# Sixteen bytes: weight rows and moving rows at another distance in SBUF

## What is computed

```python
x = x + rms_norm(mixers(rms_norm(x) @ w_in) @ w_out)
x = x + rms_norm((gelu(gate) * val) @ ffn_down)       # gate, val = split(causal_dwconv(rms_norm(x) @ ffn_up))
x = x + 0.5 * (silu(h @ w_gate) * (h @ w_up)) @ w_down   # h = rms_norm(x), twice, with d_ff = 5632
x = x + branches(attention(rms_norm(x) @ w_in_2)) @ w_out_2
```

## Time and profile before

| | |
|---|---|
| time, median of 3 runs | 3365.83 us (3364.95 to 3367.11) |
| profiled execution | 3365.98 us, of it the span 3364.2 us |
| TensorE matmuls busy | 3345.9 us, 99% |
| TensorE weight loads busy | 2933.9 us, 87% |
| VectorE busy | 2240.1 us, 67% |
| ScalarE busy | 1746.2 us, 52% |
| GpSimd busy | 533.2 us, 16% |
| granted TensorE clock | full throughout |

### The profile page before, as it was taken

One profiled execution on the slowest core, in us unless ns is written; L12 is line 12 of the kernel. 1 busy time (PEld: TensorE's weight loads), 2 busy tenths in 40 slices (PEclk: granted clock), 3 DMA queues, 4 the chain that ended last, 5 costly groups with the idle time before them and its releaser, 6 DMA issues.

```text
span 3364.2 us, 59341 instructions
## 1 busy us (share of the span) xinstructions
PE 3345.9 (99%) x19746; PEld 2933.9 (87%) x19746; DVE 2240.1 (67%) x2874; ACT 1746.2 (52%) x2588; POOL 533.2 (16%) x502
## 2 busy tenths in 40 slices
PE   9999999999999999999999999999999999999999
PEld 8888888888888888888888888888888888888888
DVE  7879587777744566556555599766687655656544
ACT  5555665555544554545444555554565554554443
POOL 0214111111100011111100066511100111111000
PEclk9999999999999999999999999999999999999999
DMA  6534555555566555555566655545556555555665
GB/s 213 163 114 154 184 169 189 190 188 187 188 193 188 178 179 192 189 190 187 187 192 189 219 175 175 189 155 159 171 193 199 190 187 193 188 188 189 186 194 175
DMA packets 176036, 616.21 MB, mean 183 GB/s; under 512 B 20912, under 2 KB 21584, under 8 KB 175568
## 3 DMA queue, kind: packets, MB, share of 16 engines
q1 hardware_dynamic: 175520, 609.84, 56.2%
q10 hardware_dynamic: 432, 5.24, 0.4%
HBM read 610.81 MB, written 4.19 MB: 183 GB/s over the span
## 4 chain that ended last, share of the span: by engine, by line
PE 94%; DVE 3%; issue 1%; ACT 1%; DMA 1%; POOL 0%; DVEq 0%; SPq 0%; POOLq 0%; ACTq 0%
PE acc L463 59%; PE acc L466 30%; DVE weights_low L313 1%; PE ps_wide L392 1%; PE acc L478 1%; ACT weights_high L306 0%; PE ps_narrow L2552 0%; PE ps_wide L2528 0%; PE acc L481 0%; DVE halves_memory L568 0%; DMA weights_raw<-in_w_in 0%; DMA x_T<-in_x 0%; DVE halves_memory L3011 0%; DMA weights_raw<-in_w_diff_branch 0%; PE ps_scale L2933 0%
## 5 line engine op out<-in xcount | busy, mean ns | idle before, releaser
L463 PE MATMUL acc<-moving_halves,weights_high 128*128 128x512 f32 x6304 | 1981.0, 395 | 1.8 <-DVE x_T L2821 1.8
L313 DVE TENSOR_TENSOR weights_low<-weights_raw,weights_high 128x1024 fp32r<-128x1024 f32 (+1 forms) x1172 | 1432.8, 1236 | 719.8 <-ACT weights_high L306 718.6
L306 ACT ACTIVATE weights_high<-weights_raw 128x1024 fp32r<-128x1024 f32 (+1 forms) x1172 | 1209.0, 1033 | 773.1 <-PE acc L466 746.7
L466 PEld LDWEIGHTS acc<-moving_halves,weights_low 128*128 128x128 f32 x6304 | 1185.0, 188 | 269.0
L466 PE MATMUL acc<-moving_halves,weights_low 128*128 128x256 f32 x6304 | 1244.0, 279 | 0.0
L463 PEld LDWEIGHTS acc<-moving_halves,weights_high 128*128 128x128 f32 x6304 | 952.4, 188 | 12.0 <-issue 9.8
L463 PE MATMUL acc<-gated_halves,weights_high 128*128 128x512 f32 x2024 | 628.0, 392 | 0.0
L562 ACT ACTIVATE cross_products<-acc 128x256 f32<-128x256 f32 x503 | 192.9, 383 | 671.2 <-PE acc L466 671.1
L466 PEld LDWEIGHTS acc<-gated_halves,weights_low 128*128 128x128 f32 x2024 | 380.1, 188 | 83.8
L585 POOL TENSOR_TENSOR stage_scratch<-unscaled,token_scale 128x256 f32<-128x256 f32 x260 | 215.2, 828 | 1287.2 <-DVE unscaled L568 807.3
L466 PE MATMUL acc<-gated_halves,weights_low 128*128 128x256 f32 x2024 | 399.4, 279 | 0.0
(11 more groups left out here) (384 smaller groups left out, 2010.7 us busy)
## 6 DMA issues: line engine op xcount, KB each, us to landing
weights_raw<-in_w_in SPq DMA_DIRECT2D x268, 512.0 KB, 3.9
weights_raw<-in_ffn_up SPq DMA_DIRECT2D x176, 512.0 KB, 4.5
weights_raw<-in_ffn_w_gate SPq DMA_DIRECT2D x176, 512.0 KB, 4.1
weights_raw<-in_ffn_w_up SPq DMA_DIRECT2D x176, 512.0 KB, 4.7
weights_raw<-in_ffn_w_down SPq DMA_DIRECT2D x160, 512.0 KB, 4.0
weights_raw<-in_ffn_down SPq DMA_DIRECT2D x80, 512.0 KB, 4.0
weights_raw<-in_w_out SPq DMA_DIRECT2D x64, 512.0 KB, 4.3
weights_raw<-in_ffn_w_down SPq DMA_DIRECT2D x32, 256.0 KB, 2.7
```

The source lines that it names most:

```text
L306: core.nc.scalar.activation(core.high[:, slot, k0:nk, :].rearrange("p a b -> p (a b)"), core.raw[:, slot, k0 * P:nk * P], ACT.Copy).then_i ...
L313: core.nc.vector.tensor_tensor(core.low[:, slot, k0:nk, :].rearrange("p a b -> p (a b)"), core.raw[:, slot, k0 * P:nk * P], core.high[:, s ...
L463: core.nc.tensor.matmul(acc[:, t % 2, :, :], core.high[:, u % SLOTS, k, :], parts[:, prod.first[t] + k0 + k, :, :], start=(k0 + k == 0), s ...
L466: core.last = core.nc.tensor.matmul(acc[:, t % 2, 0, :], core.low[:, u % SLOTS, k, :], parts[:, prod.first[t] + k0 + k, 0, :], start=False ...
```

## The change

The unused tensor ahead of the arena goes. weights_high and weights_low are allocated with 64 elements (256 bytes) more, and what the kernel uses of each begins 4 elements (16 bytes) in.

```diff
-        self.sb("before_arena", [P, 32], F32)
         self.arena_at = nc.sbuf_base
         self.arena = self.sb("arena", [P, ARENA_TILES, S], F32)
...
         self.raw = self.sb("weights_raw", [P, SLOTS, KG * P], F32)
-        self.high = self.sb("weights_high", [P, SLOTS, KG, P], F32R)
-        self.low = self.sb("weights_low", [P, SLOTS, KG, P], F32R)
+        self.high = self.past("weights_high", 4)
+        self.low = self.past("weights_low", 4)
...
+    def past(self, name, gap):
+
+        n = SLOTS * KG * P
+        flat = self.sb(name, [P, n + 64], F32R)[:, gap:gap + n]
+        return flat.rearrange("p (s k c) -> p s k c", s=SLOTS, k=KG)
```

## The result

The changed kernel took 3393.13 us (median of 6 runs, 3392.41 to 3395.43), the kernel before 3366.47 us beside it (6 runs). The ratio is 1.008, with a 95% interval of 1.0068 to 1.0092: slower by 27 us, where 11 us faster was forecast.

A forecast was written before the change was run, and what follows sets the result against it. TensorE's own matmul rate was taken as the bound, set by operand distance. From 3365.9 us, -10.7 for moving_halves and 0 for the gated, branch and mixed stages gave 3355.2 us (-0.32%), range 3315 to 3388.

The forecast's parts named there:

- What bounds the kernel: TensorE, busy 3345.9 of 3364.2 us, is held up by its own matmul rate, not by transfers, weight splits or buffers.
- the distance of the two reads: Weight-row start less moving-row start, modulo 256 bytes, goes with time per four matmuls: -64 gives 690 ns, +64 693, 0 697.
- term of -10.7 us for moving_halves: 3152 quads (two high-weight, two low-weight matmuls each) on moving_halves, going from 0.6934 to 0.6900 us each.
- I take 0.690, the nearest row: Quads at the new distance -48 were given the 0.690 us measured at -64, 16 bytes away.
- The row at 0: The 0.6966 us quad of mixed_halves at distance 0, taken as a bound above for the quad at -48.
- Rival C: No difference that can be told: distance inert (3366), or straight line from -64 to 0, 0.6916 at -48 (3362); 21%.
- nearest row is the one it has, 0: Term for mixed_halves, moving from distance 0 to +16: its quad length stays, so 0 us.
- Rival D: Slower: -48 is like 0, reads starting close together meet repeatedly; 3385, or 3400 with quads of 0.70; 22%.
- Rival B: Quads stay at 0.68 us, shorter than any row's mean: 3311, or 3333 half way at 0.685; 19%.
- The reading of the earlier trace: On gated_halves at -64, low-pair steps of 0.70 and 0.68 us were read as two alternating quad lengths averaging 0.690.
- Rival E: The 16-byte start makes VectorE's split runs so dear, from 0.60 us each, that VectorE is the bound: 3673; 2%.
- The rule of the Trainium skill: Two independent SBUF read ports, weight loads steal no bandwidth from running matmuls: the sum would be 0, the time 3365.8 us.

## Why the prediction was wrong

- **What bounds the kernel** was right: no wait of TensorE grew, the whole loss is in the rate of its matmuls, and no other engine holds it up.
- **That the distance of the two reads goes with the rate** was right where rows start at multiples of 64, and is now more than a reading of three points: distance 0 gave 0.697 and 3382 us where 3385 was worked out, and -64 for all stages but w_out gave 3356.4 where the sum of the prediction gave 3355.2. That it alone sets the rate is not so, by the two lengths in one run at -48 and at -96. Its term of -10.7 us for moving_halves at 0.690 is confirmed, for -64.
- **The step that failed** is "I take 0.690, the nearest row". At -48 the quad is 0.700 and not 0.690. The term for moving_halves is then +20.8 and not -10.7 us, and the gated and branch stages cost +12.8 where 0 was put. A row 16 bytes away is no guide: -64, -48, -32 and -16 give 0.690, 0.700, 0.693 and 0.703. The row at 0 was no bound from above either, since it gives 0.697. Rival C's straight line from -64 to 0 is met at -32 and missed at -48, where it had 0.6916.
- **mixed_halves** "nearest row is the one it has, 0" failed in the same way, with 0.7064 at +16; it is 1.3 us.
- **Rival D** had the sign and, in its longer form with 0.70 per quad, nearly the size: 3400 was written for it, and 3393 came. Its mechanism did not hold: it made -48 like 0, and -48 is worse than 0. **Rival B**, that the reads could settle on 0.68 alone, was seen at no place.
- **The reading of the earlier trace rows** behind both, and behind the bound from below, was wrong. The steps of 0.70 and 0.68 are those from low pair to low pair. From long pair to long pair the same timeline has 0.69 each time, from 1000.25 on:

```profile
1000.94 0.62 PE L463 MATMUL acc<-gated_halves,weights_high 128*128 128x512 f32 x2
...
1001.63 0.62 PE L463 MATMUL acc<-gated_halves,weights_high 128*128 128x512 f32 x2
...
1002.32 0.62 PE L463 MATMUL acc<-gated_halves,weights_high 128*128 128x512 f32 x2
```

  The alternation is thus one of where the low pairs lie between the long ones, and not of one quad of 0.68 and one of 0.70. That D's 0.70 is what -48 gives is luck.
- **Rival E**, dearer work for VectorE and ScalarE on rows that start 16 bytes in, is refuted: 1235 and 1032 ns.
- **The range** reached to 3388 and gave what lies above it, the case of 0.70, a tenth of the chance. The stages with other TensorE work gave 6.6 us back that the sum by quads did not know of.
- **The rule of the Trainium skill** (TensorE: Matmul & The Clock Gate, Part 2), that a weight load doesn't steal read bandwidth from the running matmul, would have given 3366. The runs don't bear that out: the start of the high rows or of the low ones, moved by 16 bytes, changed the time by 26 and by 9 us. That the two reads hold each other up is the plainest reading, but no row shows a collision as such.
- **What stays open**: why odd multiples of 16 are mostly long (-80, -48, -16, +16, +80) and +48 was not, and what decides between two lengths where the distance and both starts modulo 256 are the same. Starts modulo more than 256 were not tried. The steady pattern itself differs between stages of the changed kernel that have the same rate. On moving_halves at 600 us the long pairs start every 0.70 us, and at 1500 us, in a later product's stage, in steps of 0.71, 0.69 and 0.70:

```profile
600.34 0.62 PE L468 MATMUL acc<-moving_halves,weights_high 128*128 128x512 f32 x2
...
601.04 0.62 PE L468 MATMUL acc<-moving_halves,weights_high 128*128 128x512 f32 x2
...
1500.10 0.63 PE L468 MATMUL acc<-moving_halves,weights_high 128*128 128x512 f32 x2
...
1500.81 0.62 PE L468 MATMUL acc<-moving_halves,weights_high 128*128 128x512 f32 x2
...
1501.50 0.63 PE L468 MATMUL acc<-moving_halves,weights_high 128*128 128x512 f32 x2
...
1502.20 0.63 PE L468 MATMUL acc<-moving_halves,weights_high 128*128 128x512 f32 x2
```

These steps are near the rounding of the view. The single starts have 700 ns each time at 600 us, and 701, 695 and 704 ns in turn at 1500 us. A pattern into which the reads fall, each interval starting where the last one left them, would explain this, the two lengths at one distance, the stretches that keep their length and the failed sums by interval. That a length persists is shown; that colliding reads make it is argued, not shown.

## What to carry to other kernels

Where TensorE waits for nothing and still runs under its column rate, the start addresses of the weight rows and the moving rows are worth a scan: over the 18 versions here, before and after among them, this kernel went from 3356 to 3419 us with the same instructions. It must be a scan, in steps of 16 bytes, since a place 16 bytes away is no guide and high and low rows can't be tuned apart. One run measures several distances if stages differ in theirs, but one stage is not enough for a distance: two runs had 0.700 and 0.707 in two stages that differ in nothing named here. Read a stage's rate from first and last starts over hundreds of matmuls; their mean durations and busy times showed 395 against 397 ns and 99% against 100%.

## What was not expected of the hardware

- With the low rows alone 16 bytes off the distance -64, the quad is 0.7067 in place of 0.690, and the kernel takes 3419 us in place of 3356.
- The lengths crowd on few values: 0.690, 0.693, 0.697, 0.700, 0.703, 0.707, in steps of 3.3 ns, which by the 640 ns for 1536 columns is the time of eight columns. Not all lie there: 0.702 and 0.698 were read too.
- One stage can hold two lengths side by side, 0.700 and 0.707 at -96, each kept through a whole stretch of 14 or 15 quads.
- ScalarE and VectorE did not care: their 1172 instructions each, most of them on 4 KB per partition that start 16 bytes in, lasted as long as before, to 1 ns in the mean.
